# In the head loop of a windowed attention, VectorE takes maxima ahead of low parts, and two filling steps stand ahead of the values

## The reference

```
q = rmsnorm(q.reshape(B, S, 16, 64), q_norm); k = rmsnorm(k.reshape(B, S, 2, 64), k_norm)
s = jnp.einsum('bqkgd,bjkd->bkgqj', q_blk, k_blk).astype(jnp.float32) * scale
s = jnp.where(valid, s - slopes * dist, NEG)
p = jax.nn.softmax(jnp.concatenate([s, sink], axis=-1), axis=-1)[..., :-1]
o = jnp.einsum('bkgqj,bjkd->bqkgd', p, v_blk)
```

## Time and profile before

| | us |
|---|---|
| median of 3 runs | 1438.07 (1436.55 to 1438.19) |
| profiled execution | 1436.33 |
| its span, first to last instruction | 1434.5 |
| TensorE busy | 1379.3 (96%) |
| VectorE busy | 975.0 (68%) |
| ScalarE busy | 778.4 (54%) |
| GpSimd busy | 462.9 (32%) |

### The profile page before, as it was taken

One profiled execution on the slowest core, in us unless ns is written; L12 is line 12 of the kernel. 1 busy time (PEld: TensorE's weight loads), 2 busy tenths in 40 slices (PEclk: granted clock), 3 DMA queues, 4 the chain that ended last, 5 costly groups with the idle time before them and its releaser, 6 DMA issues.

```text
span 1434.5 us, 22921 instructions
## 1 busy us (share of the span) xinstructions
PE 1379.3 (96%) x7992; PEld 1216.1 (85%) x7992; DVE 975.0 (68%) x2026; ACT 778.4 (54%) x1855; POOL 462.9 (32%) x597
## 2 busy tenths in 40 slices
PE   7999999999999999898999999999999999998989
PEld 6889889898888988787888898899888888977877
DVE  6555688887755647788564656887877556577873
ACT  7354466554544437776463535656556344377661
POOL 2221242330202123956212213422311111258660
PEclk9999999999999999999999999999999999999999
DMA  6313221113341222222262132111133413221222
GB/s 227 115 49 89 80 65 54 43 49 143 122 129 55 83 71 73 63 64 94 91 199 81 53 91 84 47 61 47 38 107 122 121 48 100 59 76 58 65 70 103
DMA packets 88674, 121.47 MB, mean 85 GB/s; under 512 B 10352, under 2 KB 58864, under 8 KB 88560
## 3 DMA queue, kind: packets, MB, share of 16 engines
q1 hardware_dynamic: 83088, 112.31, 25.3%
q10 hardware_dynamic: 5472, 7.69, 1.7%
HBM read 115.77 MB, written 4.19 MB: 84 GB/s over the span
## 4 chain that ended last, share of the span: by engine, by line
PE 67%; DVE 14%; ACT 10%; issue 4%; POOL 3%; ACTq 1%; DMA 0%; SPq 0%; DVEq 0%; POOLq 0%
PE bank L1549 20%; PE bank L1551 20%; PE bank L1550 20%; PE bank L1595 5%; ACT prob L589 4%; DVE bank L1291 4%; DVE w_lo_t L903 3%; DVE probT L911 2%; ACT w_hi L564 2%; POOL rr L1370 1%; ACT probT L571 1%; DVE nmax L1295 1%; PE bank L1555 1%; PE bank L1556 1%; ACT q_st L586 1%
## 5 line engine op out<-in xcount | busy, mean ns | idle before, releaser
L903 DVE TENSOR_TENSOR w_lo_t<-w_raw,w_hi 128x256 fp32r<-128x256 f32 (+3 forms) x494 | 286.6, 595 | 249.8 <-ACT w_hi L564 237.5
L564 ACT ACTIVATE w_hi<-w_raw 128x256 fp32r<-128x256 f32 (+3 forms) x544 | 268.7, 510 | 328.8 <-PE bank L1551 312.3
L1549 PE MATMUL bank<-w_hi,actT 128*128 128x256 f32 (+3 forms) x1120 | 361.9, 323 | 8.2 <-DVE probT L911 3.1
L1550 PE MATMUL bank<-w_lo_t,actT 128*128 128x256 f32 (+3 forms) x1120 | 359.2, 321 | 0.0
L1549 PEld LDWEIGHTS bank<-w_hi,actT 128*128 128x128 f32 x1120 | 212.4, 190 | 25.2 <-DVE w_lo_t L903 4.2
L1550 PEld LDWEIGHTS bank<-w_lo_t,actT 128*128 128x128 f32 x1120 | 212.5, 190 | 14.3
L1423 POOL TENSOR_TENSOR prob<-prob,rinv 128x256 f32<-128x256 f32 x192 | 137.2, 745 | 174.8 <-DVE rinv L1009 174.8
L1551 PE MATMUL bank<-w_hi,brlo 128*128 128x256 f32 (+1 forms) x608 | 189.0, 311 | 0.0
L589 ACT ACTIVATE prob<-bank,nmax 128x256 f32<-128x256 f32 (+2 forms) x256 | 138.4, 553 | 79.7 <-DVE nmax L1203 39.6
L1551 PE MATMUL bank<-w_hi,actT 128*128 128x512 f32 (+3 forms) x512 | 170.2, 332 | 0.0
L1549 PE MATMUL bank<-actT,w_hi 128*128 128x512 f32 x384 | 152.9, 398 | 5.5 <-ACT prob L589 3.2
(11 more groups left out here) (146 smaller groups left out, 2678.5 us busy)
## 6 DMA issues: line engine op xcount, KB each, us to landing
w_raw<-in_w_mem SPq DMA_DIRECT2D x64, 256.0 KB, 2.6
w_raw<-in_w_out SPq DMA_DIRECT2D x112, 128.0 KB, 2.1
w_raw<-in_w_b SPq DMA_DIRECT2D x112, 128.0 KB, 2.1
w_raw<-in_w_b SPq DMA_DIRECT2D x48, 256.0 KB, 2.7
w_raw<-in_w_out SPq DMA_DIRECT2D x40, 256.0 KB, 2.9
w_raw<-in_w_a SPq DMA_DIRECT2D x32, 256.0 KB, 2.7
w_raw<-in_w_a SPq DMA_DIRECT2D x64, 128.0 KB, 2.1
bias<-in_alibi ACTq DMA_DIRECT2D x28, 192.0 KB, 2.3
```

The costliest lines, as they stand in the source:

```text
L564: act.activation(w_hi[:, n % SPLIT, 0:width], w_raw[:, n % RAW, 0:width], ACT.Copy).then_inc(w_hi_done, 1)
L903: dve.tensor_tensor(w_lo_t[:, n % SPLIT, 0:width], w_raw[:, n % RAW, 0:width], w_hi[:, n % SPLIT, 0:width].bitcast(fp32), ALU.subtract).th ...
L1549: nc.tensor.matmul(out, lhs[0], rhs[0], start=start, stop=False, skip_group_check=skip)
L1550: nc.tensor.matmul(out, lhs[0], rhs[1], start=False, stop=False, skip_group_check=skip)
```

## The change

VectorE takes the maxima of h+2 first and then the low parts of the transposes of h, which before stood at the end of the head ahead of it; queries and keys go to the end of its head. All engines now have two filling steps (one in head 15) at the first place, ahead of values, and at most one at the second. On TensorE queries and keys stand behind the values. ScalarE does exponentials, then the sink's, then issues the bias load, then the output's half; queries and keys stand behind the second filling place. GpSimd gets a number of weight tiles per head from `POOL_SPLITS` (the last ones of a head's steps) where it had all of the second place; three memory branches move to head 4 and behind other work of the head. Five costs of the bank planner are new.

```diff
-WINDOW_FILL = [(1, 2)] * 4 + [(1, 1)] * 2 + [(1, 2)] * 5 + [(1, 1)] * 4 + [(1, 0)]
+WINDOW_FILL = [(2, 1)] * 4 + [(2, 0)] * 2 + [(2, 1)] * 5 + [(2, 0)] * 4 + [(1, 0)]
+POOL_SPLITS = [1] * 6 + [2] * 5 + [1] * 5
-SPLIT_MEM_AT = {4: (8, 9), 5: (10, 11)}
+SPLIT_MEM_AT = {4: (8, 9, 10), 5: (11,)}
...
-            "bqT": (0.44, True, 2.2, 0.8), "bkT": (0.44, True, 1.8, 0.8), "bS": (0.39, False, 3.5, 0.8), "bPT": (0.36, True, 1.5, 0.6),
-            "bO": (1.18, True, 2.0, 0.7), "out": (2.7, False, 0.8, 0.65)}
+            "bqT": (0.44, True, 3.0, 0.8), "bkT": (0.44, True, 3.0, 0.8), "bS": (0.39, False, 3.3, 0.7), "bPT": (0.36, True, 3.0, 0.6),
+            "bO": (1.18, True, 1.5, 0.7), "out": (2.7, False, 0.8, 0.65)}
...   plan
                 fill(stream, WINDOW_FILL[h][0])
+                take([("bO", L, h)])
                 if h % 2 == 0 and h + 4 < HB:
                     take([("bqT", L, h // 2 + 2)])
                 if h + 3 == HB // 2:
                     take([("bkT", L, 1)])
-                take([("bO", L, h)])
-                first = steps[-1][2] + SPLIT
                 fill(stream, WINDOW_FILL[h][1])
-                late_split[L, h] = (first, steps[-1][2] + SPLIT)
+                late_split[L, h] = (steps[-1][2] + SPLIT - POOL_SPLITS[h], steps[-1][2] + SPLIT)
...   ScalarE, b_exp
-                            if h + 2 < HB:
-
-                                act.dma_start(bias[:, h % 2, :], alibi[h + 2]).then_inc(bias_in[h % 2], 16)
-                            act.activation(esink[:, h % 2, :], nmax[:, h % 2, :], ACT.Exp, bias=sinks[:, h:h + 1]).then_inc(esink_ready, 1)
                             for s, blocks in enumerate(SHARED):
...
+                            act.activation(esink[:, h % 2, :], nmax[:, h % 2, :], ACT.Exp, bias=sinks[:, h:h + 1]).then_inc(esink_ready, 1)
+                            if h + 2 < HB:
+
+                                act.dma_start(bias[:, h % 2, :], alibi[h + 2]).then_inc(bias_in[h % 2], 16)
...   ScalarE, head loop
+                            fill(WINDOW_FILL[h][0])
+                            if h + 2 < HB:
+                                b_exp(h + 2)
+                            b_low(h)
                             for j in SPLIT_MEM_AT.get(h, ()):
                                 branch_hi(j, ("mO", L, j - 8))
-                            fill(WINDOW_FILL[h][0])
+                            fill(WINDOW_FILL[h][1])
                             if h % 2 == 0 and h + 4 < HB:
                                 b_q(h // 2 + 2)
                             if h + 3 == HB // 2:
                                 b_k(1)
-                            b_low(h)
-                            if h + 2 < HB:
-                                b_exp(h + 2)
-                            fill(WINDOW_FILL[h][1])
                             if h + 1 < HB:
                                 b_pt(h + 1)
...   VectorE, head loop
-                        b_pt(0)
                         b_p(1)
                         for h in range(HB):
+                            if h + 2 < HB:
+                                b_max(h + 2)
+                            b_pt(h)
                             if h == B_BARE:
                                 chunk_end()
                             fill(WINDOW_FILL[h][0])
+                            b_sum(h)
                             if h + 2 < HB:
-                                b_max(h + 2)
+                                b_p(h + 2)
+                            fill(WINDOW_FILL[h][1])
                             if h % 2 == 0 and h + 4 < HB:
                                 b_q(h // 2 + 2)
                             if h + 3 == HB // 2:
                                 b_k(1)
-                            b_sum(h)
-                            fill(WINDOW_FILL[h][1])
-                            if h + 2 < HB:
-                                b_p(h + 2)
-                            if h + 1 < HB:
-                                b_pt(h + 1)
...   GpSimd, head loop
-                            for j in SPLIT_MEM_AT.get(h, ()):
-                                branch_lo(j)
                             for n in range(*LATE_SPLIT[L, h]):
...
                                 late_scale(*LATE_Q[h])
+                            for j in SPLIT_MEM_AT.get(h, ()):
+                                branch_lo(j)
...   TensorE, head loop
                             fill(WINDOW_FILL[h][0])
+                            b_o(h)
                             if h % 2 == 0 and h + 4 < HB:
                                 b_q(h // 2 + 2)
                             if h + 3 == HB // 2:
                                 b_k(1)
-                            b_o(h)
                             fill(WINDOW_FILL[h][1])
```

## The result

The changed kernel takes 1450.62 us (median of 4 runs, 1447.97 to 1453.46) against 1437.31 (1436.29 to 1438.19) of the kernel before: ratio 1.0093, 95% interval 1.0072 to 1.0114. It is slower by 13.3 us, where I had forecast 7 less. The profiled execution took 1453.46 us, 1.8 over its span.

A forecast was written before the change was run, and what follows sets the result against it. TensorE, busy 1379.3 of 1434.5 us, bounds the kernel, with VectorE and ScalarE alternating in the head loops. Heads summed to -3.8 us per loop, -7.6 in all: 1428.7 profiled, 1430 as median; range 1415 to 1443.

The forecast's parts named there:

- Part 1: VectorE, head loops: maxima ahead of low parts make the negated maximum ready at E+2.8 instead of E+6.8 (head 2).
- E: Time zero within a head: the start of the score matmuls of h+2, which end at E+1.3.
- Part 4: Queries and key at the head's end: late copies delay next scores, 4.5 us per loop (0 to 7), mostly heads 2, 4, 5.
- the third sign: Head loops: the forecast is wrong if maxima start later than 1.5 us behind their scores.
- Part 2: TensorE, head loops: two filling steps ahead of values, E+1.3 to E+4.1, cover the low parts; cost about nothing.
- Part 3: ScalarE, head loops: exponentials end at E+5.1, so TensorE's waits for them go; nothing to -11.5 us per loop.
- Part 5: New accumulators in front steps wait for low parts in heads 0, 6, 7, 10, 11, 13: +6.3 us per loop (0 to +11.4).
- Part 6: GpSimd takes fewer weight tiles in heads 0 to 3, VectorE four more: cost nothing, -0.4 to +0.4 us per loop.
- the cost that stood apart: VectorE's negations blocked beside GpSimd's multiplies: up to 2.8 us a loop, left out of the sum.
- (c): Rival, slower: VectorE falls behind, new pairs wait 3.0 or 1.7 us, +6.9 per loop, 1452 us; chance 0.19.
- (a): Rival: TensorE sets the pace, new pairs find free banks, queries stay covered; 23 us gained, 1415 us; chance 0.16.
- (b): Rival, a wash: new-pair waits and query tails cancel the exponentials' 11.5 us; 1437 us; chance 0.15.

The follow-up runs named there:

- e7: Changed kernel with one filling step ahead of the values, the rest behind, as in the kernel before: 1458.10 us.
- e4: Kernel before, with only ScalarE's exponentials moved ahead of the sink's term and the next bias load: 1425.71 us.
- e9: Changed kernel with ScalarE's sink term and bias load ahead of the exponentials again: 1452.74 us.
- e2: Changed kernel with queries and key ahead of the second filling place on ScalarE and VectorE, TensorE's order kept: 1446.58 us.
- e1: Changed kernel with VectorE's low parts ahead of the maxima again in heads 0, 6, 7, 10, 11 and 13: 1429.22 us.
- e5: Changed kernel with VectorE's low parts ahead of the maxima in every head: 1449.54 us.
- e12: Changed kernel with queries and key ahead of the values on all engines, and low parts first in heads 0, 6 and 10: 1421.40 us.
- e8: Kernel before, with four waits put into TensorE's order, one per layer, behind VectorE's scratch writes: ratio 1.0150, 1460.80 us.

## Why the prediction was wrong

**Part 1, maxima ahead of low parts: right in ten of the fourteen heads, late in heads 0, 3, 5 and 9.** I had maxima from E+0.7, the negated maximum at E+2.8 and the first low part done at E+3.4. In the ten heads maxima begin at E+0.73 to E+0.93. In heads 3, 5 and 9 they begin at E+1.75, E+3.24 and E+2.03, since these heads' own scores wait for queries (part 4). VectorE in head 0, where E is 555.25:

```profile
555.72 1.10 DVE L904 TENSOR_TENSOR w_lo_t<-w_raw,w_hi 128x256 fp32r<-128x256 f32 x3 [2.70 <-ACT w_hi L565]
...
557.04 0.57 DVE L1292 CUSTOM_DVE_ANT_0 bank<-bank,bias 128x384 f32<-128x384 f32 x1
...
558.98 0.41 DVE L1296 TENSOR_SCALAR nmax<-mx,sinks 128x4 f32<-128x4 f32 x1
559.30 1.61 DVE L912 TENSOR_TENSOR probT<-bank,probT 128x384 fp32r<-128x384 f32 x3
```

Three weight tiles and the reciprocal of head 1 still stood in the queue, so maxima began at E+1.8, and low parts at E+4.05. This is the third sign that I had named for a wrong forecast, maxima later than 1.5 us behind their scores, and it came true in these four heads of both loops.

**Part 2, two steps cover the low parts: right.** The values wait for them 0.9 us in all, and e7 shows 9.9 without the cover.

**Part 3, ScalarE: right, and without the effect that I gave it.** The 11.5 us went to zero. But e4 takes 6.5 of the 11.5 out of a loop's waits by ScalarE's order alone, and e9 shows that this order is worth nothing measurable in the changed kernel, where maxima come early: I had counted the order and the early maxima as one gain, and in good part they are two ways to the same one.

**Part 4, queries and key: right in place, 5.6 us against 4.5.** The waits stand inside or ahead of the scores that follow heads 2, 4, 5 and 8 (588.03, 606.15, 615.14, 646.97), the first three the heads that I named, and the longest, 2.32 us, behind head 4, where I had 2.5. e2 takes 3.2 of the 4.4 for queries away, but other waits ahead of the same scores take 2.1 of it back. (On head 4: one memory branch moved there from head 5, which makes three.)

**Part 5, new accumulators: the place right in all six heads, the size short.** Forecast 2.2, 2.2, 2.2 and three times 0.8, 9.0 together; measured 3.32, 2.28, 3.06 in heads 0, 6 and 10 and 0.58, 0.94, 1.02 in heads 7, 11 and 13, 11.2 together, within the bounds. Head 6 came as forecast. Head 0 is over it by the 1.1 us by which its maxima were late, head 10 by the negation, as follows.

**Part 6 and the cost that stood apart: the negation was held four times a loop.** In heads 2, 4, 8 and 10 it took 1.36, 1.36, 1.12 and 1.20 us in both loops, each time beside GpSimd's gate multiply (L1520) and ending within 0.1 us of that one's end. In head 10:

```profile
656.72 1.20 DVE L1296 TENSOR_SCALAR nmax<-mx,sinks 128x4 f32<-128x4 f32 x1
```

```profile
656.64 1.26 POOL L1520 TENSOR_TENSOR gate<-gate,o_pair 128x512 f32<-128x512 f32 x1
```

Its mean is 0.64 us over the 14 of the loop, where it was 0.49: 2.0 us a loop on VectorE, against the 2.8 that I had left out of the sum. Where it reaches TensorE can be read in head 10: negation begins at E+2.68 as in head 6 (E+2.67), takes 0.8 us longer, the low parts come as much later, and the new pair waits 3.06 us for 2.28. In heads 2, 4 and 8 it stands ahead of the queries' low halves of part 4; that it lengthened those waits is likely and not tested.

**The step that failed** is the sum itself: it added waits as if each cost its length. Parts 4 and 5 were short by 1.1 and 2.2 us a loop, which moves -3.8 to -0.5; what took it on to +8.6 (half of the 17.2 us of span) is for the most part the clock, 15.5 us over the run or 7.7 a loop, a term that stood in none of my bounds; 1.4 us a loop are left, of which 0.9 are waits ahead of values, which part 2 had at nothing. Without the clock the time would still not have been a gain: 1453.5 of the profiled execution less 15.5 is 1438.0, against 1436.3 before. So the clock made it slower, and the short sizes of parts 4 and 5 had already taken the forecast's gain. The head durations of layer 1 show it: heads 0, 5, 6 and 10, where the four falls are, took 14.18, 12.25, 12.20 and 14.21 us where I had 10.4, 8.1, 10.4 and 10.3; the other nine took 74.2 in sum where I had 74.0 (which hides head 4, 7.6 for 9.2, and head 9, 9.1 for 7.8). Two of the forecast's own signs, heads 6 and 10 under 9 us or heads 11 to 13 over 8.5, looked for other errors; the third, late maxima, did come true, and it points to waits that were too short in the sum, not to the clock.

**The rivals.** (c) named 1452, and its time came, with 19% on it, but its mechanism only in part: the point from which it was to decide, the first bank of low parts free later than E+4.0, was passed in heads 0 and 10 (about E+4.6 and E+4.4; E+3.5 in head 6), in head 10 by the held negation that it named, and the waits there, 3.32 and 3.06 us, are its 3.0. But it had 21.1 us of waits a loop, and there were 16.8; the rest was the clock. That the time fits is luck. (a), banks found free and queries covered, is refuted by the first rows of the waits. (b), at 1437, is nearest to what the waits alone would have made, 1438.0 (above).

## What to carry to other kernels

Ask of each wait in TensorE not only for its sum but for its length: a dozen of 1 us cost 12 us, four of 3 us cost 12 and, as an estimate from these runs (15 of 18 waits of 2.8 us or more came with a fall, and a fall took 1.4 to 3.1 us of TensorE's work), some 5 to 10 more. An order is set by what the next step takes: where a new accumulator takes the bank just read, its release goes first, elsewhere the chain of the next head does (e1 against e5). And before a large reordering, move what stands right ahead of the late instruction; here two instructions moved gave 12.6 of the 17 us to be had.

## What the runs showed of the hardware

The granted clock fell to 0.50, never to a level between (0.57, 0.68 and 0.91 are windows with the change inside), within a wait or up to 1.8 us behind it, stayed there for 3.4 to 6.8 us, and was back 3 to 6 us behind the wait's end. The Trainium skill (TensorE: Matmul & The Clock Gate, The HAM clock gate) says the same of the two levels: the throttled state is the default, activity releases it. The Trainium skill (the same page, A second HAM failure mode: psum-queue depth-cycling) has frequent short idles between groups of matmuls bring the lower clock too. e5 has this in small: waits of 0.84, 0.63 and 0.94 us between 640.0 and 644.1, and no longer one near, are followed by a clock of 0.50 from 644.7 to 648.1, and the same in layer 3 from 1361.5 on. It isn't the rule here: e12 is idle 43.1 us, in its head loop in waits of at most 1.4, at a clock of 1.00 throughout.

Which wait brings the fall isn't a matter of its length alone, and this stays open. Over all fourteen profiles, without the first 20 us, 15 of 18 waits of TensorE of 2.8 us or more came with a fall, 18 of 29 from 2.0 to 2.8 us, and 10 of 33 from 1.3 to 2.0 us. The same wait of the same kernel goes both ways within one execution: 3.32 us in head 0 of e7 without a fall in layer 1, 3.34 with one in layer 3; 2.32 us at 606.15 of the changed kernel with a fall in layer 1, 2.30 without in layer 3; and e2's 3.07 and 3.05 above. In the kernel before a wait of 2.56 us ahead of 661.40 has none, in e8, at the same place of the order, 2.55 ahead of 671.38 has.

At the start of a run the recorded clock can't be relied on. It is 1.00 from the first matmul on, but the 128x512 matmuls of the changed kernel take 0.63 us each from 13.1 to 15.3 us and 0.40 from 16.1 on, and in the kernel before 0.40 from 12.4 on. 0.77 against 0.47 us, for the first of a row, is what the lower clock makes of such a matmul in head 0 too. Runs of either order start either way (e4 slow, e12 fast); by these durations it costs an estimated 1.6 us in the changed kernel, and is in no clock sum above.

The four executions of the changed kernel show the clock in their times: mean clocks of 0.988, 0.989, 0.991 and 0.994 go with 1453.46, 1451.19, 1450.04 and 1447.97 us. The costs of the bank planner weren't tried by themselves.
